# Attention scores in one VectorE pass: sum with distances, row minimum and sink together, scores divided by the slope

## The chip, the cores and the metric

The kernel runs on one core of a Trainium2 chip. A core has five engines that run on their own and wait for each other by semaphores: TensorE (PE, matrix multiply into PSUM), VectorE (DVE), ScalarE (ACT), GpSimd (POOL) and SyncE (SP, which issues DMAs). The metric is the device time of one execution in microseconds, lower is better.

## What is computed

Two transformer-like blocks on 256 tokens of width 1024, all in fp32. The change lies in the second block, in its sliding-window attention: 16 query heads of 64 share 2 key and value heads, a bias falls linearly with the distance between query and key, and each head has a sink value that takes part in the softmax as one more logit.

```python
def swa_mixer(h, w_qkv, sinks, w_o):
    ...
    s = jnp.einsum('bnqkgd,bnskd->bnkgqs', q, kb).astype(jnp.float32) * (HD ** -0.5)
    ...
    dist = BLOCK + qi - kj
    mask = (dist >= 0) & (dist < WINDOW) & (kpos >= 0)
    slopes = alibi_slopes(SWA_HEADS).reshape(1, 1, KV, G, 1, 1)
    bias = -slopes * dist.astype(jnp.float32)[None, :, None, None]
    logits = jnp.where(mask[None, :, None, None], s + bias, NEG)
    m = jnp.maximum(jnp.max(logits, axis=-1, keepdims=True), sink)
    p = jnp.exp(logits - m)
    probs = p / (jnp.sum(p, axis=-1, keepdims=True) + jnp.exp(sink - m))
    o = jnp.einsum('bnkgqs,bnskd->bnqkgd', probs.astype(vb.dtype), vb)
    return o.reshape(B_, T, SWA_HEADS * HD) @ w_o
```

BLOCK and WINDOW are 128, the slope of head n (from 1 to 16) is 2^(-n/2), and dist is the distance in tokens.

## The kernel before

Each engine has its own program, written out in order, and waits for others on counting semaphores. All weights come through one pipeline in units of 128 x 1024: SyncE loads a unit (`raw`), ScalarE copies it to a rounded high part (`whi`, line 1152), GpSimd takes the difference as the low part (`wlo`, lines 514 to 520), and TensorE does three matmuls for each product (lines 545 to 547: high by high, and the two cross terms). Six slots of each kind form the ring, so ScalarE makes the split of a unit some five units ahead.

The attention is done in eight head pairs t = 0 to 7, in a software pipeline over all engines. In order, for pair t:

- TensorE, scores (lines 1022, 1023): two heads, each 128 x 256 for the second block of tokens against both key blocks, and 128 x 128 for the first block, into the two PSUM banks `bank[0]`, `bank[1]`. All pairs use the same two banks, so the scores of pair t wait until VectorE has released those of pair t - 1 (`free("score", t)`).
- VectorE, `scores(t)` (lines 2182 to 2199): for each head one operation over 384 elements writes slope x distance minus score into `lg` (so the softmax is computed on negated values); then, behind the reciprocal of pair t - 1 (`scales(t - 1)`, line 2178), two row minima (lines 2197, 2198) over the scores and the sink column beside them, which raise `att_neg`. A masked place holds -1e30 in the table of negated distances, `ndist`.
- ScalarE (line 1562): four exponentials with their row sums, bias from the minima. Before, it has written the negated sinks into `lg` (line 1547, `att_sink`, three pairs ahead). After it, high part of an output (line 1569) and, for some t, a weight unit (line 1152).
- GpSimd (line 505): two multiplications by the reciprocals, placed in its program between weight units (lines 519, 520): pair 0, unit, pair 1, unit, pairs 2, 3 and 4, unit, pairs 5 and 6, unit, pair 7.
- TensorE, transposes (line 1038) into two PSUM banks; VectorE copies them (line 2206, `pt`); TensorE multiplies by the values (lines 1049 to 1051); ScalarE and VectorE split the result in high (line 1569) and low part (line 2212, `att_low`, which raises `att_ready`).

VectorE's order for step t is: scores(t) with the reciprocal of t - 1 in it, the copy of t - 2, the low part of t - 4. For steps 2 and 3, half of the second group of queries follows (`queries(1, ...)`, line 2154, 128 x 512). At step 7 the low part of pair 3 stands ahead of the scores. TensorE's order for step t is: scores of t, a unit of the output projection for t = 6, 8, 9 and 10 (`o_unit`, lines 545 to 547 with `ya_hi`, `ya_lo`), transposes of t - 2, values of t - 3. The first projection unit waits for the low part of pair 1, the second for that of pair 3.

`link(ins)` raises a semaphore with the instruction and has VectorE wait for it before its next one; `settle` is that wait alone.

Of the kernel before, what the change touches and what calls it, by code (L numbers as in the profile page):

```python
# [8 lines left out]
ALU = mybir.AluOpType  # L9
ACT = mybir.ActivationFunctionType  # L10
AX_X = mybir.AxisListType.X

P = 128
T = 256
# [12 lines left out]
AH = 16  # L27
AD = 64
# [10 lines left out]
C_NEG1T = C_NEG + len(LEVELS) * P  # L39
C_PICK = C_NEG1T + P  # L40
C_DIST = C_PICK + 3 * 192 + P // 2
C_ALL = C_DIST + 3 * P
EXP_TABLES = "exp_and_others"
LOG_TABLES = "natural_log_exp_and_others"
SILU_TABLES = "silu_and_others"
# [87 lines left out]
LG = 3 * P + 2  # L133
# [8 lines left out]
def build(nc, a, consts, out):  # L142
    with ExitStack() as ctx:
# [10 lines left out]
        con = sb("con", [P, C_ALL])  # L154
# [11 lines left out]
        with ExitStack() as ph:  # L166
            lg = sb("lg", [P, 3, 2 * LG], stack=ph)
# [9 lines left out]
        neg1t = con[:, C_NEG1T:C_NEG1T + P]  # L177
        pick = {s: con[:, C_PICK + 192 * i:C_PICK + 192 * (i + 1)].bitcast(I32) for i, s in enumerate((1, 4, 16))}
        pick_half = con[:, C_PICK + 3 * 192:C_DIST].bitcast(I32)
        ndist = con[:, C_DIST:C_DIST + 3 * P]  # L180


        with ExitStack() as ph:
# [45 lines left out]
        root = sb("root", [P, T])  # L229
        with ExitStack() as ph:  # L230
            qa = sb("qa", [P, KT, T], stack=ph)
            ka = sb("ka", [P, 2, T], stack=ph)
# [3 lines left out]
            st_att = sb("st_att", [P, 2, 2, 4], stack=ph)  # L236
# [118 lines left out]
        att_in = sem("att_in")  # L355
        att_neg = sem("att_neg")
# [1256 lines left out]
        def _(vec):  # L1613
            raised = {}

            def link(ins, sem_=vec_chain):

                ins.then_inc(sem_, 1)
                settle(sem_)

            def settle(sem_):

                raised[id(sem_)] = raised.get(id(sem_), 0) + 1
                vec.wait_ge(sem_, raised[id(sem_)])
# [524 lines left out]
            def queries(c, parts=range(2)):  # L2149

                group_ready("q_att", c)
                bank = pair_of("q_att", c)
                for b in parts:
                    vec.scalar_tensor_tensor(qa[:, 4 * c + 2 * b:4 * c + 2 * b + 2, :], bank[b][:, :].rearrange("p (k t) -> p k t", k=2),
                        AD ** -0.5, root[:, :].unsqueeze(1).broadcast_to([P, 2, T]), ALU.mult, ALU.mult).then_inc(att_in, 1)
                    settle(att_in)
                if b == 1:
                    free("q_att", c)

# [2 lines left out]
            queries(0)  # L2162
            group_ready("kv_att", 0)
            bank = pair_of("kv_att", 0)
            vec.tensor_tensor(ka[:, :, :], bank[0][:, :].rearrange("p (k t) -> p k t", k=2),
                root[:, :].unsqueeze(1).broadcast_to([P, 2, T]), ALU.mult).then_inc(att_in, 1)
            settle(att_in)
            link(vec.tensor_scalar(va[:, 0, :], bank[1][:, 0:P], mv[:, 0, 2:3], None, ALU.mult))
            vec.tensor_scalar(va[:, 1, :], bank[1][:, P:2 * P], mv[:, 1, 2:3], None, ALU.mult).then_inc(att_in, 1)
# [11 lines left out]
            def scores(t):  # L2181

                group_ready("score", t)
                bank = pair_of("score", t)
                par = t % 2
                if t - 2 > 0:
                    vec.wait_ge(att_t, t - 2)
                rows = lg[:, t % 3, :].rearrange("p (h c) -> p h c", h=2)
                for j in range(2):
                    blocks = bass.AP(lg, (t % 3) * 2 * LG + j * LG, [[3 * 2 * LG, P], [P + 1, 3], [1, P]])  # L2190
                    link(vec.scalar_tensor_tensor(blocks, ndist.rearrange("p (b c) -> p b c", b=3), -2.0 ** (-8.0 * (2 * t + j + 1) / AH),
                        bank[j][:, 0:3 * P].rearrange("p (b c) -> p b c", b=3), ALU.mult, ALU.subtract))
                free("score", t)
                if t > 0:
                    scales(t - 1)
                vec.wait_ge(att_sink, t + 1)
                link(vec.tensor_reduce(st_att[:, par, 0, 0:2], rows[:, :, 0:2 * P + 1], AX_X, ALU.min))
                vec.tensor_reduce(st_att[:, par, 0, 2:4], rows[:, :, 2 * P + 1:LG], AX_X, ALU.min).then_inc(att_neg, 1)
                settle(att_neg)

            def probs_turned(t):

# [123 lines left out]
def shape_constants():  # L2326

    import numpy as np

    i, j = np.arange(P)[:, None], np.arange(P)[None, :]  # L2330
    out = np.zeros((P, C_ALL), np.float32)
    out[:, C_ID:C_ID + P] = i == j
    out[:, C_UPTO:C_UPTO + P] = i <= j
    out[:, C_AFTER:C_AFTER + P] = i > j
    out[:, C_ONES:C_ONES + P] = 1
    for n, s in enumerate(LEVELS):
        below = (i // s % 2 == 1) & (j // s == i // s - 1)
        out[:, C_NEG + n * P:C_NEG + (n + 1) * P] = np.where(below, -1, 0)
        if s == 1:
            out[:, C_NEG1T:C_NEG1T + P] = np.where(below.T, -1, 0)  # L2340
    for n, s in enumerate((1, 4, 16)):
        same = np.arange(P)[:, None] // (4 * s) == np.arange(P // (4 * s))[None, :]
        block = np.arange(P) // s % 4
        rows = np.stack([block == b for b in (0, 0, 0, 1, 2, 1)], 1)
        mask = (same[:, :, None] & rows[:, None, :])[:, :, :, None].repeat(s, 3)
        out[:, C_PICK + 192 * n:C_PICK + 192 * (n + 1)] = mask.reshape(P, 192)
    out[:, C_PICK + 3 * 192:C_DIST] = np.arange(P)[:, None] < 64
    key = np.arange(2 * P)[None, :]
    dist = P + i - key
    out[:, C_DIST:C_DIST + 2 * P] = np.where((dist >= 0) & (dist < P), -dist, -1e30)  # L2350
    out[:, C_DIST + 2 * P:C_DIST + 3 * P] = out[:, C_DIST + P:C_DIST + 2 * P]
    return out


# [24 lines left out]
```

## Time and profile before

| | |
|---|---|
| median of 3 runs | 984.41 us (984.31 to 984.83) |
| the profiled execution | 984.0 us, its span 982.2 us |
| TensorE busy | 953.8 us, 97% of the span |
| GpSimd busy | 675.4 us, 69% |
| ScalarE busy | 499.4 us, 51% |
| VectorE busy | 454.7 us, 46% |

The span is from the first to the last instruction of the profile; the time of an execution is a little longer. Busy is the time in which an engine works on an instruction; an engine that is nearly always busy sets the time, and a change elsewhere counts only where this engine waits for it. The granted clock is that of TensorE, 1.0 for 2.4 GHz and 0.5 for 1.2 GHz.

### The profile page before, as it was taken

To read this page: it belongs to the slowest core of one execution; us is meant where nothing else is said; L and a number is where in the kernel's file an instruction comes from. 1 tells how busy PE (TensorE), PEld (TensorE's weight loads), DVE (VectorE), ACT (ScalarE), POOL (GpSimd) and SP (SyncE) were. 2 spreads that over 40 slices of the span, in tenths; PEclk is the share of its full clock that TensorE was granted. 3 is DMA by queue.
4 is the path that set the end of the run, shared out by engine and by line. 5 is a ranking of instruction groups with operands and counts; after the bars stand their busy time and mean duration, and the time that the engine had idled before them with its cause. 6 is when DMAs were issued, how large, how long until landed. Compare 5 with 4: busy or idle time off the path is not lost.

```text
span 982.2 us, 17653 instructions
## 1 busy us (share of the span) xinstructions
PE 953.8 (97%) x6878; PEld 893.2 (91%) x6878; DVE 454.7 (46%) x831; ACT 499.4 (51%) x702; POOL 675.4 (69%) x486
## 2 busy tenths in 40 slices
PE   6999999999999999999999999999997999999997
PEld 6999999999998889999999999888896789998886
DVE  3458753377443242666565565516537352221003
ACT  3675342573225466555566546456557346554331
POOL 4886644467555797866665676668787549889983
PEclk9999999999999999999999999999999999999999
DMA  8989858869634565644444544455572137656641
GB/s 243 167 205 108 177 103 85 157 108 101 141 106 127 182 200 167 192 129 150 132 127 129 151 130 141 135 184 175 150 235 87 49 111 226 195 171 200 206 131 43
DMA packets 131243, 146.30 MB, mean 149 GB/s; under 512 B 11022, under 2 KB 95960, under 8 KB 131160
## 3 DMA queue, kind: packets, MB, share of 16 engines
q1 hardware_dynamic: 129176, 140.64, 56.8%
q10 hardware_dynamic: 1984, 4.53, 1.4%
q8 instruction: 54, 0.88, 0.4%
q14 instruction: 29, 0.24, 0.1%
HBM read 144.10 MB, written 1.05 MB: 148 GB/s over the span
## 4 chain that ended last, share of the span: by engine, by line
PE 82%; DVE 5%; POOL 4%; issue 3%; ACT 2%; DMA 2%; SPq 1%; DVEq 0%; ACTq 0%; POOLq 0%
PE dense L545 22%; PE dense L546 21%; PE dense L547 21%; PE bank L907 3%; DMA raw<-in_w_in_even_dram 2%; POOL wlo L520 2%; PE bank L803 2%; PE bank L806 2%; POOL wlo L519 2%; PE bank L821 1%; ACT whi L1152 1%; DVE cv L1738 1%; PE bank L896 1%; PE dense L614 1%; PE bank L964 1%
## 5 line engine op out<-in xcount | busy, mean ns | idle before, releaser
L520 POOL TENSOR_TENSOR wlo<-raw,whi 128x512 fp32r<-128x512 f32 (+1 forms) x263 | 411.8, 1572 | 30.8 <-ACT whi L1152 30.8
L519 POOL TENSOR_TENSOR wlo<-raw,whi 128x512 fp32r<-128x512 f32 x199 | 258.9, 1301 | 240.2 <-ACT whi L1152 240.0
L1152 ACT ACTIVATE whi<-raw 128x1024 fp32r<-128x1024 f32 x264 | 276.3, 1058 | 274.4 <-PE dense L547 241.0
L545 PE MATMUL dense<-x_hi,whi 128*128 128x256 f32 x1232 | 360.9, 293 | 9.6 <-POOL wlo L514 4.8
L547 PE MATMUL dense<-x_hi,wlo 128*128 128x256 f32 x1232 | 348.9, 283 | 0.0
L546 PE MATMUL dense<-x_lo,whi 128*128 128x256 f32 x1232 | 348.8, 283 | 0.0
L545 PEld LDWEIGHTS dense<-x_hi,whi 128*128 128x128 f32 x1232 | 236.5, 192 | 13.2 <-issue 6.6
L546 PEld LDWEIGHTS dense<-x_lo,whi 128*128 128x128 f32 x1232 | 236.6, 192 | 1.8 <-issue 1.7
L547 PEld LDWEIGHTS dense<-x_hi,wlo 128*128 128x128 f32 x1232 | 236.2, 192 | 0.0
L545 PE MATMUL dense<-whi,ya_hi 128*128 128x512 f32 x192 | 78.5, 409 | 1.8 <-issue 1.8
L547 PE MATMUL dense<-whi,ya_lo 128*128 128x512 f32 x192 | 75.7, 394 | 0.0
L546 PE MATMUL dense<-wlo,ya_hi 128*128 128x512 f32 x192 | 75.5, 393 | 0.0
L1738 DVE SCALAR_TENSOR_TENSOR cv<-dense,colA,cv 128x255 f32<-128x255 f32 (+2 forms) x72 | 34.7, 482 | 27.1 <-ACT cv L1225 24.5
L545 PEld LDWEIGHTS dense<-whi,ya_hi 128*128 128x128 f32 x192 | 36.4, 189 | 10.0 <-issue 3.2
L547 PEld LDWEIGHTS dense<-whi,ya_lo 128*128 128x128 f32 x192 | 36.4, 189 | 7.9
L546 PEld LDWEIGHTS dense<-wlo,ya_hi 128*128 128x128 f32 x192 | 36.4, 190 | 7.2 <-issue 0.5
L1142 ACT ACT_TABLE_LOAD x32 | 41.1, 1283 | 2.4 <-PEq L2366 1.2
L545 PE MATMUL dense<-whi,x_hi 128*128 128x256 f32 (+1 forms) x144 | 40.9, 284 | 0.0
L546 PE MATMUL dense<-wlo,x_hi 128*128 128x256 f32 (+1 forms) x144 | 40.6, 282 | 0.0
L547 PE MATMUL dense<-whi,x_lo 128*128 128x256 f32 (+1 forms) x144 | 40.5, 282 | 0.0
L545 PE MATMUL dense<-whi,yb_hi 128*128 128x512 f32 x96 | 38.2, 398 | 0.3 <-POOL wlo L520 0.3
L547 PE MATMUL dense<-whi,yb_lo 128*128 128x512 f32 x96 | 37.4, 390 | 0.0
(324 smaller groups left out, 1429.4 us busy)
## 6 DMA issues: line engine op xcount, KB each, us to landing
raw<-in_w_in_odd_dram SPq DMA_DIRECT2D x64, 512.0 KB, 3.6
raw<-in_w_in_even_dram SPq DMA_DIRECT2D x32, 512.0 KB, 10.2
raw<-in_w_in_even_dram SPq DMA_DIRECT2D x64, 256.0 KB, 5.6
raw<-in_mlp_w_up_dram SPq DMA_DIRECT2D x32, 512.0 KB, 3.7
raw<-in_mlp_w_down_dram SPq DMA_DIRECT2D x32, 512.0 KB, 4.5
raw<-in_w_out_even_dram SPq DMA_DIRECT2D x16, 512.0 KB, 3.9
raw<-in_w_pl_gate_dram SPq DMA_DIRECT2D x16, 512.0 KB, 4.6
raw<-in_w_out_odd_dram SPq DMA_DIRECT2D x16, 512.0 KB, 3.9
```

The costliest lines, as they stand in the source:

```text
L519: pool.tensor_tensor(wlo[:, slot, 0:half], unit_slot(u)[:, 0:half], whi[:, slot, 0:half].bitcast(F32), ALU.subtract)
L520: pool.tensor_tensor(wlo[:, slot, first:2 * half], unit_slot(u)[:, first:2 * half], whi[:, slot, first:2 * half].bitcast(F32), ALU.subtrac ...
L545: pe.matmul(out_, lh, rh, start=start, stop=False, skip_group_check=True)
L546: pe.matmul(out_, lh, rl_, start=False, stop=False, skip_group_check=True)
L547: return pe.matmul(out_, ll, rh, start=False, stop=stop, skip_group_check=True)
L614: last = pe.transpose(bank[:, j * P:(j + 1) * P], xtok[:, t, k * P:(k + 1) * P], ident)
L803: last = pe.matmul(A[:, o], unit(LT[:, g, :], u), unit(XN[:, g, :], u), start=True, stop=True)
L806: last = pe.matmul(B[:, u * 64:(u + 1) * 64], unit(XT[:, g, :], u), even_odd(unit(EL[:, g, :], u), lv, 0), start=True, stop=True)
L907: last = pe.matmul(low_banks[:, u * T:u * T + 192], tokens_of(hk, p % 2, u // 2, u % 2), six, start=True, stop=True)
L1142: act.preload_act_table_set(name)
L1152: act.activation(whi[:, u % NSPL, :], unit_slot(u), ACT.Copy).then_inc(hi_done, 1)
L1738: link(vec.scalar_tensor_tensor(o, bank[:, i * T:(i + 1) * T - back], colA[:, w:w + 1], o, ALU.mult, ALU.add), conv_done if back == 3 else ...
```

## The change

The two operations a pair that made the biased scores and the two that took the minima become four operations, `tensor_tensor_reduce`, each of which writes (distance + score) x slope, and gives the minimum of what it wrote with the sink as the first value. For that the scores must come from TensorE as minus the score divided by the slope: the queries are multiplied by 2^t more than before, which takes one operation for each of four tiles where two tiles shared one, and the keys by a column of the constants, `nslope` (-sqrt 2 or -2 by the head within the pair). The table of distances loses its sign. Each of the new operations writes 256 elements (second block of tokens) or 128 (first block).

```diff
-C_ALL = C_DIST + 3 * P
+C_ALL = C_DIST + 3 * P + 1
...
-        ndist = con[:, C_DIST:C_DIST + 3 * P]
+        dist = con[:, C_DIST:C_DIST + 3 * P]
+        nslope = con[:, C_DIST + 3 * P:C_DIST + 3 * P + 1]
...
-                    vec.scalar_tensor_tensor(qa[:, 4 * c + 2 * b:4 * c + 2 * b + 2, :], bank[b][:, :].rearrange("p (k t) -> p k t", k=2),
-                        AD ** -0.5, root[:, :].unsqueeze(1).broadcast_to([P, 2, T]), ALU.mult, ALU.mult).then_inc(att_in, 1)
-                    settle(att_in)
+                    for j in range(2):
+                        t = 4 * c + 2 * b + j
+                        link(vec.scalar_tensor_tensor(qa[:, t, :], bank[b][:, j * T:(j + 1) * T], AD ** -0.5 * 2.0 ** t, root[:, :], ALU.mult, ALU.mult),
+                             att_in if j else vec_chain)
...
-            vec.tensor_tensor(ka[:, :, :], bank[0][:, :].rearrange("p (k t) -> p k t", k=2),
-                root[:, :].unsqueeze(1).broadcast_to([P, 2, T]), ALU.mult).then_inc(att_in, 1)
+            vec.scalar_tensor_tensor(ka[:, :, :], bank[0][:, :].rearrange("p (k t) -> p k t", k=2), nslope,
+                root[:, :].unsqueeze(1).broadcast_to([P, 2, T]), ALU.mult, ALU.mult).then_inc(att_in, 1)
...
-                rows = lg[:, t % 3, :].rearrange("p (h c) -> p h c", h=2)
+                vec.wait_ge(att_sink, t + 1)
                 for j in range(2):
-                    blocks = bass.AP(lg, (t % 3) * 2 * LG + j * LG, [[3 * 2 * LG, P], [P + 1, 3], [1, P]])
-                    link(vec.scalar_tensor_tensor(blocks, ndist.rearrange("p (b c) -> p b c", b=3), -2.0 ** (-8.0 * (2 * t + j + 1) / AH),
-                        bank[j][:, 0:3 * P].rearrange("p (b c) -> p b c", b=3), ALU.mult, ALU.subtract))
+                    slope = 2.0 ** (-8.0 * (2 * t + j + 1) / AH)
+                    row = (t % 3) * 2 * LG + j * LG
+                    for tile, first, n in ((0, 0, 2), (1, 2, 1)):
+                        o = bass.AP(lg, row + first * (P + 1), [[3 * 2 * LG, P], [P + 1, n], [1, P]])
+                        cols = slice(first * P, (first + n) * P)
+                        sink = bass.AP(lg, row + P + tile * (P + 1), [[3 * 2 * LG, P], [1, 1]])
+                        last = vec.tensor_tensor_reduce(o, dist[:, cols].rearrange("p (b c) -> p b c", b=n),
+                                                        bank[j][:, cols].rearrange("p (b c) -> p b c", b=n), slope, sink, ALU.add, ALU.min,
+                                                        accum_out=st_att[:, par, 0, 2 * tile + j:2 * tile + j + 1])
+                        link(last, att_neg if (j, tile) == (1, 1) else vec_chain)
                 free("score", t)
                 if t > 0:
                     scales(t - 1)
-                vec.wait_ge(att_sink, t + 1)
-                link(vec.tensor_reduce(st_att[:, par, 0, 0:2], rows[:, :, 0:2 * P + 1], AX_X, ALU.min))
-                vec.tensor_reduce(st_att[:, par, 0, 2:4], rows[:, :, 2 * P + 1:LG], AX_X, ALU.min).then_inc(att_neg, 1)
-                settle(att_neg)
```

The order of VectorE's instructions for step 4, with the semaphores that each waits for, is before:

```order
L2191 SCALAR_TENSOR_TENSOR lg<-con,dense 128x3x128 [waits att_in,att_t,turned]
L2191 SCALAR_TENSOR_TENSOR lg<-con,dense 128x3x128 [waits vec_chain]
L2178 RECIPROCAL rsum<-st_att 128x4 [waits vec_chain,att_scale,att_exp]
L2197 TENSOR_REDUCE st_att<-lg 128x2 [waits att_sink,att_root]
L2198 TENSOR_REDUCE st_att<-lg 128x2 [waits vec_chain]
L2206 COPY pt<-bank 128x768 [waits att_o,att_t,att_neg]
L2212 TENSOR_TENSOR ya_lo<-bank,ya_hi 128x256 [waits att_hi,att_pt]
```

And now (ISA with `lg,st_att` is the new operation, ISA with `st_att` alone the read of its accumulator):

```order
L2198 ISA lg,st_att<-con,dense,lg 128x2x128 [waits att_in,att_sink,att_t,turned]
L2198 ISA st_att 128x1
L2198 ISA lg,st_att<-con,dense,lg 128x128 [waits vec_chain]
L2198 ISA st_att 128x1
L2198 ISA lg,st_att<-con,dense,lg 128x2x128 [waits vec_chain]
L2198 ISA st_att 128x1
L2198 ISA lg,st_att<-con,dense,lg 128x128 [waits vec_chain]
L2198 ISA st_att 128x1
L2180 RECIPROCAL rsum<-st_att 128x4 [waits att_neg,att_scale,att_exp]
L2211 COPY pt<-bank 128x768 [waits att_o,att_t,att_root]
L2217 TENSOR_TENSOR ya_lo<-bank,ya_hi 128x256 [waits att_hi,att_pt]
```

Four instructions became eight, and the reciprocal moved from the middle of the score work to behind it. The program of the other engines is the same instruction by instruction, but for one DMA of the constants on ScalarE's queue, whose rows have 1025 elements instead of 1024.

The second place is the step before the scores of step 4, where half a group of queries is taken. Before:

```order
L2206 COPY pt<-bank 128x768 [waits att_t,att_neg]
L2154 SCALAR_TENSOR_TENSOR qa<-dense,root 128x512 [waits split_used,att_pt]
L2191 SCALAR_TENSOR_TENSOR lg<-con,dense 128x3x128 [waits att_in,att_t,turned]
```

And now:

```order
L2211 COPY pt<-bank 128x768 [waits att_t,att_root]
L2157 SCALAR_TENSOR_TENSOR qa<-dense,root 128x256 [waits split_used,att_pt]
L2157 SCALAR_TENSOR_TENSOR qa<-dense,root 128x256 [waits vec_chain]
L2198 ISA lg,st_att<-con,dense,lg 128x2x128 [waits att_in,att_sink,att_t,turned]
```

One operation over two tiles became two, one after the other.

## Rows read from the trace of the kernel before

**Rows 1.** The page: span, busy time of each engine, and the chain's shares.
```profile
span 982.2 us, 17653 instructions
...
PE 953.8 (97%) x6878; PEld 893.2 (91%) x6878; DVE 454.7 (46%) x831; ACT 499.4 (51%) x702; POOL 675.4 (69%) x486
...
PE 82%; DVE 5%; POOL 4%; issue 3%; ACT 2%; DMA 2%; SPq 1%; DVEq 0%; ACTq 0%; POOLq 0%
```

**Rows 2.** Busy time by stage; columns: length, engines, clock, DMA share, GB/s.
```profile
740.00:758.00 18.00, 12.33 (x101) 9.85 (x100) 15.33 (x28) 12.51 (x40) 14.25 (x15) 0.97 0.25 81
```

**Rows 3.** Timeline of VectorE; columns: start, duration (of all in xN), instruction, idle before.
```profile
741.84 0.69 DVE L2154 SCALAR_TENSOR_TENSOR qa<-dense,root 128x512 f32<-128x512 f32 x1
...
747.21 1.15 DVE L2191 SCALAR_TENSOR_TENSOR lg<-con,dense 128x384 f32<-128x384 f32 x2 [0.21 <-DVE qa L2154]
748.57 0.18 DVE L2178 RECIPROCAL rsum<-st_att 128x4 f32<-128x4 f32 x1 [0.21 <-DVE lg L2191]
748.78 0.69 DVE L2197 TENSOR_REDUCE st_att<-lg 128x2 f32<-128x514 f32 x1
749.51 0.42 DVE L2198 TENSOR_REDUCE st_att<-lg 128x2 f32<-128x258 f32 x1
749.96 0.96 DVE L2206 COPY pt<-bank 128x768 f32<-128x768 f32 x1
...
755.15 0.42 DVE L2212 TENSOR_TENSOR ya_lo<-bank,ya_hi 128x256 fp32r<-128x256 f32 x1
...
763.03 1.15 DVE L2191 SCALAR_TENSOR_TENSOR lg<-con,dense 128x384 f32<-128x384 f32 x2
```

**Rows 4.** Timeline of TensorE from the first projection unit on.
```profile
755.68 0.47 PE L545 MATMUL dense<-whi,ya_hi 128*128 128x512 f32 x1 [1.83 <-issue]
...
757.42 0.63 PE L545 MATMUL dense<-whi,ya_hi 128*128 128x512 f32 x1
...
759.99 0.93 PE L1038 MATMUL bank<-con,lg 128*128 128x128 f32 x6
...
767.52 0.82 PE L1038 MATMUL bank<-con,lg 128*128 128x128 f32 x6
...
773.88 0.88 PE L1038 MATMUL bank<-con,lg 128*128 128x128 f32 x6 [1.49 <-POOL lg L505]
```

**Rows 5.** Timeline of ScalarE and GpSimd behind the scores of pair 7.
```profile
765.84 0.51 ACT L1562 ACTIVATE lg<-lg,st_att 128x257 f32<-128x257 f32 x1 [3.37 <-DVE st_att L2198]
...
764.65 1.61 POOL L505 TENSOR_TENSOR lg<-lg,rsum 128x512 f32<-128x512 f32 x2 [5.81 <-DVE rsum L2178]
...
769.72 1.30 POOL L519 TENSOR_TENSOR wlo<-raw,whi 128x512 fp32r<-128x512 f32 x1 [3.46 <-ACT whi L1152]
...
772.22 1.61 POOL L505 TENSOR_TENSOR lg<-lg,rsum 128x512 f32<-128x512 f32 x2
```

**Rows 6.** Groups of VectorE by line (busy, mean ns), then a stretch of ScalarE's timeline.
```profile
L1738 DVE SCALAR_TENSOR_TENSOR cv<-dense,colA,cv 128x255 f32<-128x255 f32 x24 | 11.6, 483 | 25.3 <-ACT cv L1225 24.5
L2304 DVE SCALAR_TENSOR_TENSOR zt<-xtok,mv,gb 128x512 f32<-128x512 f32 x2 | 1.5, 752 | 0.6 <-ACT mv L1604 0.6
L2212 DVE TENSOR_TENSOR ya_lo<-bank,ya_hi 128x256 fp32r<-128x256 f32 x8 | 3.4, 425 | 6.3 <-ACT ya_hi L1569 6.1
...
731.72 0.51 ACT L1562 ACTIVATE lg<-lg,st_att 128x257 f32<-128x257 f32 x1 [5.07 <-DVE st_att L2198]
732.13 0.19 ACT L1562 ACTIVATION_READ_ACCUMULATOR lg<-lg,st_att 128x1 f32 x1
732.35 0.51 ACT L1562 ACTIVATE lg<-lg,st_att 128x257 f32<-128x257 f32 x1
```

**Rows 7.** VectorE's wait, the constants' first DMA, and TensorE's clock by stage.
```profile
725.45 0.69 DVE L2165 TENSOR_TENSOR ka<-dense,root 128x512 f32<-128x512 f32 x1 [8.99 <-PE dense L547]
con<-shape_constants_dram ACTq DMA_DIRECT2D x1, 64.0 KB, 3.3
757.00:758.00 1.00, 1.00 (x4) 0.50 0.00 0
```

More of the change, by code:

```diff
@@ L2349, in shape_constants @@
     dist = P + i - key
-    out[:, C_DIST:C_DIST + 2 * P] = np.where((dist >= 0) & (dist < P), -dist, -1e30)
+    out[:, C_DIST:C_DIST + 2 * P] = np.where((dist >= 0) & (dist < P), dist, 1e30)
     out[:, C_DIST + 2 * P:C_DIST + 3 * P] = out[:, C_DIST + P:C_DIST + 2 * P]
+    out[:, C_DIST + 3 * P] = np.where(np.arange(P) < 64, -2.0 ** (8.0 / AH), -2.0 ** (16.0 / AH))
     return out
```

## The prediction

> **What bounds the kernel now.** Read the page first: TensorE is busy 97% of the 982.2 us and holds 82% of the chain that ended last [rows 1]. A change on VectorE counts only where TensorE waits. The change lies between 725 and 770 us, and the busy time by stage shows that this is the one stretch where TensorE is not full: 12.33 us of 18 between 740 and 758, with VectorE busy 15.33 [rows 2].
>
> In order of time, VectorE works without a real pause from 741.84 on, in blocks of one head pair: two score operations, the reciprocal of the pair before, two row minima, the copy of turned scores, the low part of an output [rows 3]. TensorE's output projection cannot start before the low part of pair 1, which runs 755.15 to 755.57; its first matmul stands at 755.68 [rows 3, 4]. After it come the transposes of pair 4 (759.99), its values and the scores of pair 7, all back to back. VectorE takes pair 7 at 763.03, ScalarE its exponentials at 765.84, then a weight unit; GpSimd splits that unit at 769.72 and scales pair 7 only at 772.22; TensorE, idle by then, turns pair 7 at 773.88 [rows 3 to 5]. From there its work is dense. So two VectorE times set the end: when the low part of pair 1 is done, and when the minima of pair 7 are done.
>
> **The change, part by part.** One number for a pause between two linked operations: 748.78 + 0.69 to 749.51 and 749.51 + 0.42 to 749.96 leave 0.04 and 0.03; I take 0.035 us [rows 3].
>
> *Removed per pair:* two score operations and two minima. From 747.21 to 749.96 is 2.75 us, of which 748.36 (= 747.21 + 1.15) to 748.78 is the reciprocal with its pause, 0.42. Score work: 2.33 us.
>
> *Added per pair:* four operations of 256, 128, 256 and 128 elements, each with an accumulator read. Each operation has one PSUM input, one SBUF input and a per-partition scalar (the sink). The nearest row has just this make-up: 255 elements, 483 ns [rows 6]. An element costs (689 - 422)/256 = 1.04 ns, from the two minima of 514 and 258 elements [rows 3]. So 484 and 350 ns, with pauses 2 x (0.484 + 0.350 + 0.07) = 1.81 us. The read of VectorE's accumulator is in no row. Above it stands the smallest operation here, the reciprocal, 0.18 + 0.035 = 0.21. ScalarE's accumulator read is nearest in kind: 0.19 long, but it starts 0.41 after an operation of 0.51, and the next starts 0.63 after the first, so it adds 0.63 - 0.51 - 0.02 = 0.10 [rows 6]. Below that nothing but full overlap, 0. I take 0.15, between the two near rows, since each next operation waits for the read. Score work after: 1.81 + 4 x 0.15 = 2.41 us; bounds 2.21 and 2.65, and 1.81 with the reads free. That is +0.08 a pair: two passes became one, but four fixed costs became eight.
>
> *Queries:* each operation over 512 elements becomes two over 256. One with its pause is 0.69 + 0.035 = 0.73 now; two of 0.425 (the 256-element low part) with pauses are 0.92, +0.18 [rows 3, 6]. Two of them (before pairs 3 and 4) are on the path, +0.37. Those of the first half are hidden: VectorE idles 9 us behind them, until the keys' group is done [rows 7]. The keys' operation gains a scalar, about 0.06 (752 ns with a scalar against 0.69 without, at 512 elements [rows 3, 6]); the unit of query matmuls that TensorE does before the first scores hides it; without that cover it costs its 0.06.
>
> *Moved:* the reciprocal, and the release of the score banks, now come after the minima. The minima of pair 7 therefore stop waiting for a reciprocal: -0.42 on the path. The reciprocal starts 2.41 + 0.21 after the block instead of 1.36, 1.26 later. Who waits for it is GpSimd's scaling, then the transposes. For pair 6 scaling ends at 764.65 + 1.61 = 766.26 and the transposes start at 767.52 behind a projection unit: 1.26 of cover, just used up, and another 1.5 us of TensorE idle before 773.88 behind it [rows 4, 5]. For pair 3 the reciprocal would start at 748.57 + 0.45 (one block and both query parts) + 1.26 = 750.3, and scaling end 0.18 + 1.61 later, at 752.1. The banks are released at the end of block 5, near 751.9 + 2.4 = 754.4; the scores of pair 6 then take some 0.9, and the low part of pair 1 comes at 756.2 (755.57 + 0.61). Covered by 0.9. Queued on VectorE behind the four operations are the reciprocal and the copy; the sink values they wait for were written one to several pairs earlier. ScalarE's and GpSimd's order does not change.
>
> *Sum.* Blocks 3, 4 and 5 lie before the low part of pair 1: 3 x 0.08 + 0.37 = +0.61. Block 7: 0.08 - 0.42 = -0.34. Together +0.27 us; in general four times the score work less 9.37 (3 x 2.33 + 2.75 - 0.37). With 2.21 it is -0.5, with 2.65 +1.2, with free reads -2.1. The profiled execution took 984.0 (982.2 and 1.8 around it), so 984.3; the runs' median is 984.41, so 984.7 in the unit of the runs.
>
> **A rate.** The operation at 512 elements with two SBUF inputs and a scalar takes 752 ns, (512 x 1.04) + 219, so it runs at one element a cycle like the others [rows 6]. Against this stands the Trainium skill, "Vector Engine (DVE) Microarchitecture Reference", section 7 (Points that are easy to get wrong): a scalar_tensor_tensor shape with two non-bf16 SBUF sources has half the throughput, for want of a port for the accumulator. By that rule the time would be the 987.9 of the first rival; by the row it stays at 984.7. Here one source is in PSUM, and no row of before accumulates on VectorE, so the trace does not settle it.
>
> **The rivals.**
> 1. *Half rate.* The new operation takes two cycles an element. 768 elements a pair cost 0.80 us more; on four blocks 3.2, so 987.9. For it: it does three things in one pass and carries a value from element to element. Against it: the minima carry one too and run at full rate. It decides from 0.5 us a pair. This is the case of slower. Chance 0.08.
> 2. *The clock does not fall.* At 757 the granted clock went from 1.0 to 0.5, after a pause of TensorE of 1.83 us before the projection; until 759.99 the last seven matmuls of the unit, of 512 columns, stood 0.43 apart (from 757.42 to 759.99 are six), twice what they take at full clock [rows 4, 7]. In the changed kernel the pause is split by the later scores of pair 6. If the fall stays out, 7 x 0.21 = 1.5 us come off: 983.2. Chance 0.20.
> 3. *The clock falls for longer or once more,* say over the next projection unit's 12 matmuls: 12 x 0.21 = +2.5, 987.2. Pauses on TensorE grow a little everywhere. Chance 0.07.
> 4. *The reads are free:* 982.3. Against it is that each next operation waits for the read. Chance 0.06.
> 5. *The late reciprocal binds,* because GpSimd is late for the transposes: needs 2.8 us of lateness for pair 6, or 0.9 more than reckoned for pair 3, where each 0.1 above costs 0.1; about 986. Chance 0.04.
> 6. *The start.* The constants' rows get one element longer in memory, and TensorE's first transposes need the first of them. That transfer took 3.3 us [rows 7]; a tenth more is +0.3, 985.0. Chance 0.05.
>
> My forecast, clock as before and reads between 0.10 and 0.21, has 0.50: 983.9 to 985.6.
>
> **How the numbers follow.** The predicted time is 984.7. What a measurement of this kernel can tell from no change is 0.2%, 2.0 us, so the forecast and cases 2, 5 and 6 are within it. Slower takes case 1, most of case 3 and mixtures with costly reads: 0.16. Faster takes half of case 4 and case 2 with cheap reads: 0.06. Same: 0.78. The range leaves out case 1, part of 3 and part of 4: 982.8 to 986.9.
>
> **What would show it.** In the profile after: the 256-element operation 0.48 us and the 128-element one 0.35, reads near 0.15 apart; if not, case 1 or 4. Score work near 2.4 a pair. The first projection matmul near 756.3. The minima of pair 7 end 2.4 after its start. VectorE busy time about the same, TensorE's idle between the projection's third unit and pair 7's transposes still there. The clock row at 757 to 760 tells cases 2 and 3. What would make the prediction wrong is a read of over 0.3 us, a rate below one element a cycle, or a fall of the clock elsewhere.

## Result and the profile after

| | median us | lowest to highest |
|---|---|---|
| before | 984.62 | 984.31 to 987.08 (4 runs) |
| changed | 974.08 | 973.64 to 976.7 (4 runs) |

The ratio is 0.9893, with an interval of 0.9869 to 0.9917: 10.5 us faster. The prediction had 984.7 us, a range from 982.8 to 986.9, and gave "faster" 0.06. It was wrong, and by more than any case it had named.

The page of the changed kernel, against [rows 1]: the span is 10.3 us shorter, and TensorE's own busy time is 9.6 us shorter, with the same 6878 instructions. The change took no instruction from TensorE, so a wait that went away can't be the whole story.

```profile
span 971.9 us, 17687 instructions
...
PE 944.2 (97%) x6878; PEld 880.7 (91%) x6878; DVE 451.1 (46%) x867; ACT 499.6 (51%) x702; POOL 675.4 (69%) x486
```

**Where the time went.** Follow one instruction that both programs have. `root` is copied right before the first attention query, ahead of every changed operation, and once more behind the attention; its row gives both starts. Before, then after:

```profile
L2147 DVE COPY root<-bank x2: 425/425/425, 714.6 to 807.3; 128x256 f32<-128x256 f32 x2
```

```profile
L2148 DVE COPY root<-bank x2: 425/425/425, 710.3 to 799.2; 128x256 f32<-128x256 f32 x2
```

4.3 us were gained before any of the changed operations had run. Up to the second copy it is 8.1, at the end 10.3: 4.3 ahead of the attention, 3.7 to 3.8 in it, 2.2 behind it. The prediction had looked only at the middle part.

**In the attention.** VectorE's timeline of the changed kernel at step 2 (start, duration, instruction), then one whole block at step 3, against the block from 747.21 to 749.96 in [rows 3]:

```profile
732.82 0.48 DVE L2198 CUSTOM_DVE_ANT_0 lg<-con,dense,lg 128x256 f32<-128x256 f32 x1 [1.85 <-PE dense L1024]
...
738.34 0.48 DVE L2198 CUSTOM_DVE_ANT_0 lg<-con,dense,lg 128x256 f32<-128x256 f32 x1
738.75 0.08 DVE L2198 DVE_READ_ACCUMULATOR2_ANT st_att<- 128x1 f32 x1
738.87 0.35 DVE L2198 CUSTOM_DVE_ANT_0 lg<-con,dense,lg 128x128 f32<-128x128 f32 x1
739.14 0.08 DVE L2198 DVE_READ_ACCUMULATOR2_ANT st_att<- 128x1 f32 x1
739.26 0.48 DVE L2198 CUSTOM_DVE_ANT_0 lg<-con,dense,lg 128x256 f32<-128x256 f32 x1
739.66 0.08 DVE L2198 DVE_READ_ACCUMULATOR2_ANT st_att<- 128x1 f32 x1
739.78 0.35 DVE L2198 CUSTOM_DVE_ANT_0 lg<-con,dense,lg 128x128 f32<-128x128 f32 x1
740.05 0.08 DVE L2198 DVE_READ_ACCUMULATOR2_ANT st_att<- 128x1 f32 x1
740.35 0.18 DVE L2180 RECIPROCAL rsum<-st_att 128x4 f32<-128x4 f32 x1 [0.21 <-DVE st_att L2198]
740.56 0.96 DVE L2211 COPY pt<-bank 128x768 f32<-128x768 f32 x1
```

The operations last 0.48 and 0.35 us, as reckoned. But each read of the accumulator starts 0.41 (0.27) after the start of its operation, before the end that the profile gives that operation, and the next operation starts 0.12 after the read. From start to start an operation with its read takes 0.53 and 0.39, one head 0.92. The block is 2.22 long instead of 2.75; less the reciprocal's 0.42 the score work is 1.80 us, not 2.41.

TensorE's timeline after, against [rows 4]:

```profile
750.14 0.48 PE L546 MATMUL dense<-whi,ya_hi 128*128 128x512 f32 x1 [0.67 <-issue]
750.45 0.40 PE L547 MATMUL dense<-wlo,ya_hi 128*128 128x512 f32 x1
750.69 0.39 PE L548 MATMUL dense<-whi,ya_lo 128*128 128x512 f32 x1
...
753.01 0.82 PE L1039 MATMUL bank<-con,lg 128*128 128x128 f32 x6
...
765.87 0.88 PE L1039 MATMUL bank<-con,lg 128*128 128x128 f32 x6 [0.51 <-POOL lg L506]
```

The pause before the projection is 0.67 us instead of 1.83, and behind the first matmul the others of the unit stand 0.23 to 0.24 apart. The 12 matmuls take 2.87 us (750.14 to 753.01) instead of 4.31 (755.68 to 759.99). The clock stays at its upper level (1.00, 2.4 GHz) through the whole stage; before, it was 0.50 from 757 to 760 [rows 7]. Here are the stage after, with its clock in the last column but two, and the three microseconds before:

```profile
740.00:760.00 20.00, 17.20 (x138) 13.86 (x137) 15.11 (x50) 13.74 (x47) 11.82 (x14) 1.00 0.19 59
```

```profile
757.00:760.00 3.00, 3.00 (x9) 2.25 (x8) 1.26 (x3) 1.51 (x5) 1.73 (x3) 0.50 0.50 160
```

ScalarE's exponentials of pair 7 and GpSimd's scaling follow 8.0 us earlier than in [rows 5]:

```profile
757.84 0.51 ACT L1563 ACTIVATE lg<-lg,st_att 128x257 f32<-128x257 f32 x1 [2.45 <-DVE st_att L2198]
```

```profile
764.20 1.62 POOL L506 TENSOR_TENSOR lg<-lg,rsum 128x512 f32<-128x512 f32 x2
```

**Outside the attention.** A run of ordinary projection matmuls near 130 us, of before and of after (starts in the first column):

```profile
132.08 0.28 PE L547 MATMUL dense<-x_hi,wlo 128*128 128x256 f32 x1
132.20 0.28 PE L545 MATMUL dense<-x_hi,whi 128*128 128x256 f32 x1
132.32 0.28 PE L546 MATMUL dense<-x_lo,whi 128*128 128x256 f32 x1
132.44 0.28 PE L547 MATMUL dense<-x_hi,wlo 128*128 128x256 f32 x1
132.56 0.28 PE L545 MATMUL dense<-x_hi,whi 128*128 128x256 f32 x1
```

```profile
130.06 0.28 PE L546 MATMUL dense<-x_hi,whi 128*128 128x256 f32 x1
130.18 0.28 PE L547 MATMUL dense<-x_lo,whi 128*128 128x256 f32 x1
130.30 0.28 PE L548 MATMUL dense<-x_hi,wlo 128*128 128x256 f32 x1
130.41 0.28 PE L546 MATMUL dense<-x_hi,whi 128*128 128x256 f32 x1
130.53 0.28 PE L547 MATMUL dense<-x_lo,whi 128*128 128x256 f32 x1
130.65 0.28 PE L548 MATMUL dense<-x_hi,wlo 128*128 128x256 f32 x1
130.76 0.28 PE L546 MATMUL dense<-x_hi,whi 128*128 128x256 f32 x1
```

Four steps of 0.12 there, six steps in 0.70 here: 120 ns from start to start against 117, for the same matmul of the same 256 columns. There are 4080 matmuls of 256 columns with `x_hi` or `x_lo`. The one thing in the diff that can reach them is `C_ALL`: `con` has 2561 columns instead of 2560, the allocation rounds up, and in the compiled program every tile in SBUF behind `con` starts 32 bytes later in its partition. The tiles `whi` and `wlo` lie ahead of `con` and stay.

### The profile page after: what moved, and what is told of

It is laid out like the page before. It is cut to its first block, busy times and chain, and to the rows that moved or that the text cites. A ratio compares the mean times of both kernels' runs of the same rounds, so it can differ in the third digit from the quotient of the medians.

```text
span 971.9 us, 17687 instructions
## 1 busy us (share of the span) xinstructions
PE 944.2 (97%) x6878; PEld 880.7 (91%) x6878; DVE 451.1 (46%) x867; ACT 499.6 (51%) x702; POOL 675.4 (69%) x486
## 3 DMA queue, kind: packets, MB, share of 16 engines
HBM read 144.10 MB, written 1.05 MB: 149 GB/s over the span
## 4 chain that ended last, share of the span: by engine, by line
PE 85%; DVE 4%; POOL 3%; ACT 3%; DMA 2%; issue 2%; SPq 1%; DVEq 0%; ACTq 0%; POOLq 0%
PE dense L546 23%; PE dense L547 22%; PE dense L548 22%; PE bank L908 3%; DMA raw<-in_w_in_even_dram 2%; PE bank L804 2%; PE bank L807 2%; POOL wlo L521 1%; POOL wlo L520 1%; PE bank L822 1%; POOL lg L506 1%; DVE cv L1739 1%; PE bank L897 1%; ACT whi L1153 1%; PE dense L615 1%
## 5 line engine op out<-in xcount | busy, mean ns | idle before, releaser
L546 PE MATMUL dense<-x_hi,whi 128*128 128x256 f32 x1232 | 356.9, 290 | 11.1 <-POOL wlo L515 5.3
L547 PE MATMUL dense<-x_lo,whi 128*128 128x256 f32 x1232 | 344.5, 280 | 0.0
L548 PE MATMUL dense<-x_hi,wlo 128*128 128x256 f32 x1232 | 344.3, 279 | 0.0
L546 PEld LDWEIGHTS dense<-x_hi,whi 128*128 128x128 f32 x1232 | 232.4, 189 | 14.8 <-issue 7.4
L547 PEld LDWEIGHTS dense<-x_lo,whi 128*128 128x128 f32 x1232 | 232.4, 189 | 1.8 <-issue 1.7
L548 PEld LDWEIGHTS dense<-x_hi,wlo 128*128 128x128 f32 x1232 | 232.1, 188 | 0.0
```

The costliest lines, as they stand in the source:

```text
L546: pe.matmul(out_, lh, rh, start=start, stop=False, skip_group_check=True)
L547: pe.matmul(out_, lh, rl_, start=False, stop=False, skip_group_check=True)
L548: return pe.matmul(out_, ll, rh, start=False, stop=stop, skip_group_check=True)
```

## Theories

**A (addresses).** The spacing of matmuls depends on where the tiles of their two operands start; the shift of 32 bytes gives what lies outside the attention. **S (scores).** The operations give what lies in it: shorter score work, and a clock that does not fall. **Rival:** nothing but S, with the rest due to the constants' longer rows in DRAM or to chance.

## Experiments

"Spacing" below is the median distance of the starts of neighbouring matmuls in the trace: `x` for the products of moving `x_hi` or `x_lo` (256 columns) with the weights as the stationary tile, `ya` for those of the weights (moving, 512 columns) with `ya_hi` or `ya_lo` as the stationary tile (`yb` and `p` alike unless said), `ac` the same for the MLP's. "The attention stretch" runs from the start of TensorE's scores of pair 2 (736.10 before) to that of the transposes of pair 7 (773.88). Each ratio is to the kernel before on the same chip. The first four ran on one chip.

**e1_before_pad32: the shift alone.**

```diff
         con = sb("con", [P, C_ALL])
+        pad = sb("pad", [P, 8])
```

> The kernel before with nothing changed but an unused 32-byte tile behind the constants, so that every tile from colA on starts 32 bytes later, as in the changed kernel. Theory A (the time of a matmul depends on where its operands' tiles start within 64 bytes): x_hi matmuls 117 ns apart instead of 120, those with ya or yb 233 instead of 227, ac 227 instead of 234; the attention stage is reached 4.3 us earlier and the end gains another 2.4: 977.9 us, with no change inside the attention stage. Rival B (the early gain comes from the constants' longer rows in memory, from the added operation's table or from chance): 984.4 us. Rival C (the whole gain is that of the score operations): 984.4 us.

Measured: 980.85 us (977.23 to 983.86, 10 runs; before 985.74), ratio 0.9948 (0.9928 to 0.9968); the profiled span 975.4, 6.8 below before. Spacings 117, 233 to 234, 227, as in the changed kernel. The root copies' stretches: 4.3 us shorter up to the first, 2.2 from the second to the end; the attention stretch 37.82 us against 37.79. Theory A holds for what lies outside, without one changed operation. The spacings add up, too: 4080 matmuls at 3 ns less make 12.2 us, 912 with `ya`, `yb` and `p` at 6 more 5.5 us, and 186 with `ac` at 7 less 1.3 us, together 8.0 us less; TensorE's busy time in this run is 945.8 us, 8.0 less than before.

**e2_after_nopad: the operations alone.** `nslope` in a tile of its own behind all others, written by two memsets; the constants at 2560 columns.

```diff
-C_ALL = C_DIST + 3 * P + 1
+C_ALL = C_DIST + 3 * P
...
+        nslope = sb("nslope", [P, 1])
...
+            for n in range(2):
+                link(vec.memset(nslope[64 * n:64 * n + 64, :], -2.0 ** (8.0 * (n + 1) / AH)))
```

> The changed kernel with the tiles where they were before: the keys' factor stands in a tile of its own behind all others, set by two small VectorE operations, and the constants have their old size. Theory A: matmuls 120, 227 and 234 ns apart as before, the stage reached at its old time, 3.7 us saved between pair 2's scores and pair 7's transposes (2.1 from the shorter score work, 1.5 from the clock that does not fall): 980.7 us. Rival B or C: 974.1 us, or B with the gain in the constants' rows: 980.7 with the new spacings kept.

Measured: 981.15 us (980.22 to 983.1), 0.9956 (0.9943 to 0.997). Spacings as before; the attention stretch 34.16 us, 3.6 shorter; clock not fallen. In the profile the first copy of `root` comes 0.7 us later than before, so nothing is gained ahead of the attention. Theory S holds for the middle. The product of both ratios, 0.9904, lies within the interval of the change.

**e3_before_row2561: the constants' rows alone.** In DRAM one column more, in SBUF the layout of before; the last of the constants' DMAs still moves 1024 elements a row, not 1025 as in the changed kernel.

> The kernel before with the constants' rows in memory 2561 elements long instead of 2560, all tiles on chip as before. Theory A: 984.4 us, or up to 0.65 more, since the first unit's matmul stood 0.65 later in the changed kernel (12.03 against 11.38). Rival B (longer rows bring the early gain): 980 or less.

Measured: 985.23 us, 0.9996 (0.9982 to 1.0009). The longer rows make no difference that can be told from noise. Nor does the one element more in that DMA: e1, without it, reaches the first copy of `root` at 710.26 us and the changed kernel at 710.27. With e1 and e3 the rival falls.

**e4_before_pad64: twice the shift** (`pad` of 16 floats, 64 bytes).

> The kernel before with an unused 64-byte tile behind the constants, so that every later tile moves by 64 bytes. Theory A with a period of 64 bytes: 984.4 us and the spacings of before (120, 227, 234 ns). If the period is 128 bytes or longer, or any shift acts, the x_hi spacing is 117 or another value than 120.

Measured: 983.49 us, 0.9983 (0.9968 to 0.9997). Spacings 118, 233, 233, where before has 120, 227, 234: a shift by 64 bytes does not give the old spacings back, so 64 bytes is no period of the effect.

**e5_after_layout and e6_before_layout: a layout by design.** I thought that 512 columns go fast from a multiple of 128 bytes: `x` moved by 32 bytes, `ya`, `yb`, `p`, `ac` to multiples of 256; with the operations of after and of before. These and the next two ran on a second chip.

```diff
+        pad_x = sb("pad_x", [P, 8])
         x_hi = sb("x_hi", [P, KT, T], F32R)
         x_lo = sb("x_lo", [P, KT, T], F32R)
+        pad_y = sb("pad_y", [P, 24])
         ya_hi = sb("ya_hi", [P, KT, T], F32R)
...
+        pad_ac = sb("pad_ac", [P, 8])
```

> The changed score operations (keys' factor in a tile of its own) with a layout chosen by what the first runs showed: x_hi and x_lo start 32 bytes past a multiple of 128, ya, yb, p and ac start on a multiple of 128. Theory A (the start within 128 bytes sets the spacing: a 256-column moving operand is faster off it, a 128-column stationary operand under 512 moving columns is faster on it): 117 for x_hi, 227 for ya, yb, p and ac at once. From 984.4: 4080 matmuls x 3 ns = 12.2 off, 192 x 6.5 = 1.3 off, 0.8 of it lost where TensorE waits, and 3.6 off in the attention stage: 968 us. Rival D (x_hi and ya share one property that can't be had for both, such as the distance between the two operands): no better than 974.

> The same layout with the score operations of before. Theory A: 984.4 - 12.7 = 971.7 us, 3.6 above the kernel with the changed score operations. Rival D: not below 977.

Measured: 976.37 us (0.9901, 0.9881 to 0.992) and 979.87 (0.9933, 0.9912 to 0.9955), before 985.47. Spacings 117, 232, 232. Expected were 227 for `ya` and `ac`, and 968 and 971.7 us, so my form of theory A fell: a multiple of 128 is not enough. That the two stand 3.5 us apart confirms S once more.

**e7_before_whi32: the weights moved too.** `whi` and `wlo` 32 bytes later, everything behind them at another offset again.

```diff
+        pad_w = sb("pad_w", [P, 8])
         whi = sb("whi", [P, NSPL, SPLK * COLS], F32R)
         wlo = sb("wlo", [P, NSPL, SPLK * COLS], F32R)
         con = sb("con", [P, C_ALL])
+        pad_c = sb("pad_c", [P, 24])
```

> The kernel before with whi and wlo alone starting 32 bytes past a multiple of 128 and everything else as it was. It exchanges the roles: for x_hi the stationary operand is off and the moving one on, for ya the moving one off and the stationary one on. Theory A: x_hi slower than 120 ns (the stationary operand costs 3 or more), ya 227 or less; 984.4 + 12 or more = 997 us. Rival D (only the difference of the two starts counts): x_hi 117 and ya 233, 978 us.

Measured: 990.36 us (988.8 to 993.57), 1.0048 (1.0026 to 1.0071), slower than before. The distances of `x` spread from 115 to 126 ns here, with a mean of 120 as before; `ya` and `ac` stand 234 to 235 apart. Neither theory A (997 us) nor D as it was worded (`x` 117, 978 us) gave this. The slower `ya`, `yb` and `p` account for it: 912 matmuls times 6 to 7 ns are about 6 us, and 4.9 were measured (990.36 - 985.47).

**e8_after_nopad_slow: score work made long again.** e2 with one more VectorE operation of 384 elements per pair, into a tile that nothing reads. It makes the score work 2.42 us, which is what the prediction had thought.

```diff
+                        if (j, tile) == (1, 0):
+                            link(last)
+                            link(vec.tensor_tensor(idle[:, :], dist, bank[0][:, 0:3 * P], ALU.add))
+                            continue
```

> The changed kernel with the old addresses and one more VectorE operation a pair, between the last two score operations: distances plus scores of 384 elements into a tile that nobody reads, 0.59 us with its pause. It makes the score work 1.83 + 0.59 = 2.42 us a pair, what the prediction had put at 2.41. Theory S (the prediction's chain was right and only the accumulator read was mis-sized): four times 0.59 = 2.4 us back, so 983.1, and another 1.5 us if the granted clock falls again at the first projection unit: 984.6. Rival E (other waits set the stage and the score work is hidden): 981.2, as without it.

Measured: 985.21 us (983.47 to 988.15), 0.9993 (0.9979 to 1.0007): with the predicted score work and the old addresses the time is that of before. The attention stretch is 36.96 us, 2.8 above e2, where the work alone makes 4 x 0.6 = 2.4. That the remaining 0.4 is the clock's is likely, but no run separates it: the clock fell here, elsewhere than before, at a pause of 2.13 us, and stayed at 1.00 at the projection, whose pause is now split into parts of 0.38 and 0.81 us by the scores of pair 6. TensorE's row at the fall, and the clock by stage:

```profile
744.72 1.54 PE L1040 MATMUL bank<-con,lg 128*128 128x128 f32 x6 [2.13 <-POOL lg L507]
```

```profile
745.00:748.00 3.00, 3.00 (x18) 2.49 (x17) 2.63 (x8) 1.73 (x7) 3.00 (x3) 0.50 0.29 111
```

**What the starts had in common.** By now it looked as if the start of the activations' tile (`x`, `ya`, `yb`, `p`, `ac`) counted against that of the weights' tile, both modulo 256 bytes. Three more kernels, with the changed kernel beside them, ran on a third chip (before 985.72 us).

**e9_before_all32: everything shifted together**, `pad_w` of 8 floats ahead of `whi` and nothing else.

> The kernel before with 32 unused bytes per partition right ahead of whi, so that whi, wlo and every tile behind them start 32 bytes later together (whi, wlo, x_hi, ya_hi, yb_hi, p_hi at 160 modulo 256, ac_hi at 128). If what counts is how the moving tile starts against the weights' tile (theory D), x and ya keep the spacing of before (120 ns for 256 columns, 227 ns for 512) and the time is 984 to 985 us. If what counts is the moving tile's own start (theory M), x goes to 117 ns, ya, yb and p to 233, ac to 227, and the time is that of e1, 978 to 981 us. If it is the weights' start alone, x and ya stay at 120 and 233 ns as in e7, about 990 us.

Measured: 985.72 us (983.8 to 986.88), 0.9995 (0.9981 to 1.001); spacings 120, 227, 234. `x_hi`, `ya_hi` and `ac_hi` start just where they do in the changed kernel, and their matmuls behave as before. Not the start of one tile counts but how the two stand to each other (form D of the expectation). The other two forms fell.

**e10_after_layout2 and e12_before_layout2: the best of each**, with the changed operations (from e2) and with those of before. Both have these three tiles:

```diff
+        pad_x = sb("pad_x", [P, 8])
         x_hi = sb("x_hi", [P, KT, T], F32R)
         x_lo = sb("x_lo", [P, KT, T], F32R)
+        pad_y = sb("pad_y", [P, 56])
         ya_hi = sb("ya_hi", [P, KT, T], F32R)
...
+        pad_ac = sb("pad_ac", [P, 8])
```

> The changed operations in a layout that takes the better spacing of each tile as seen so far: whi, wlo at 128 modulo 256 as before, x_hi and x_lo 32 bytes later (160), ya, yb and p back at 128, ac at 128. Expected by both forms D and M: x 117 ns, ya, yb, p and ac 227 ns. Against the changed kernel 912 matmuls of 512 columns become 6 ns shorter, 5.5 us of TensorE, so 966 to 970 us if TensorE is the bound there, and 974 if other work bounds those stages. If only the whole shift by 32 bytes of everything behind con brings the gain, it is 978 or more.

> The operations of before in the layout of e10. If addresses and operations add up, it stands above e10 by what the operations alone brought in the other two pairs (984.6 to 981.2 and 979.9 to 976.4, that is 3.5 us): 970 to 974 us, faster than the changed kernel or equal to it without any of its operations. If the gain of addresses is only that of e1, it is 978 to 981.

**e11_after_again: the changed kernel on that chip.**

> The changed kernel itself, on the same chip as e10 and e12, to compare with them: 974 us, ratio to before 0.989.

Measured: e10 970.87 us (969.34 to 972.49), 0.9839 (0.9811 to 0.9866); e12 974.42 (972.36 to 976.1), 0.9873 (0.9845 to 0.9902); e11 974.99 (974.46 to 979.44), 0.9892 (0.9853 to 0.9931). e10 and e12 lie 0.9 and 0.4 us above the ranges expected by form D (966 to 970 and 970 to 974), and well under the 978 us and more expected without it. e10 is the fastest kernel of the study, 4.1 us under the changed one, and all of its runs are below the lowest of e11. e12 has not one changed operation and is as fast as the change: three unused tiles do as much. Operations and addresses add up again, 3.6 us between e10 and e12.

TensorE is busy for 940.5 us in e10, against 944.2 in the changed kernel and 953.8 before. Groups of matmuls by shape (count, busy us, mean ns) of before, after, e9 and e10:

```profile
L546 PE MATMUL dense<-x_lo,whi 128*128 128x256 f32 x1232 | 348.8, 283 | 0.0
L546 PE MATMUL dense<-wlo,yb_hi 128*128 128x512 f32 x96 | 37.4, 389 | 0.0
L546 PE MATMUL dense<-wlo,ac_hi 128*128 128x512 f32 x62 | 24.5, 395 | 0.0
```

```profile
L547 PE MATMUL dense<-x_lo,whi 128*128 128x256 f32 x1232 | 344.5, 280 | 0.0
L547 PE MATMUL dense<-wlo,yb_hi 128*128 128x512 f32 x96 | 37.9, 395 | 0.0
L547 PE MATMUL dense<-wlo,ac_hi 128*128 128x512 f32 x62 | 24.1, 389 | 0.0
```

```profile
L547 PE MATMUL dense<-x_lo,whi 128*128 128x256 f32 x1232 | 349.0, 283 | 0.0
L547 PE MATMUL dense<-wlo,yb_hi 128*128 128x512 f32 x96 | 37.4, 389 | 0.0
L547 PE MATMUL dense<-wlo,ac_hi 128*128 128x512 f32 x62 | 24.5, 395 | 0.0
```

```profile
L550 PE MATMUL dense<-x_lo,whi 128*128 128x256 f32 x1232 | 344.6, 280 | 0.0
L550 PE MATMUL dense<-wlo,yb_hi 128*128 128x512 f32 x96 | 37.4, 389 | 0.0
L550 PE MATMUL dense<-wlo,ac_hi 128*128 128x512 f32 x62 | 24.1, 389 | 0.0
```

In these four kernels each kind of matmul has two values, 3 ns apart for 256 columns and 6 for 512. The changed kernel won on `x`, lost on `yb` and won on `ac`; e10 has the better value in all three, e9 the old one in all three.

All layouts side by side (start modulo 256 bytes; spacing in ns):

| kernels | whi | x | ya, yb, p | ac | x spacing | ya | ac |
|---|---|---|---|---|---|---|---|
| before, e2, e3, e8 | 128 | 128 | 128 | 96 | 120 | 227 | 234 |
| after, e1, e11 | 128 | 160 | 160 | 128 | 117 | 233 to 234 | 227 |
| e4 | 128 | 192 | 192 | 160 | 118 | 233 | 233 |
| e5, e6 | 128 | 160 | 0 | 0 | 117 | 232 | 232 |
| e7 | 160 | 0 | 0 | 224 | 120 (115 to 126) | 234 | 235 |
| e9 | 160 | 160 | 160 | 128 | 120 | 227 | 234 |
| e10, e12 | 128 | 160 | 128 | 128 | 117 | 227 | 227 |

With equal starts the 512-column matmuls are at their best and the 256-column ones at their worst; every other distance tried is worse for the former, and for the latter better, but for e7, where the mean is as it was.

## Why the prediction was wrong, point by point

**The failed step** is the scope of the sum: it had terms for the operations and, of the one new constants column, only "The constants' rows get one element longer in memory". It priced the DMA (which costs nothing, e3) and put at nothing, without a reason, the 32 bytes by which every later tile moves. They are as large a part as the operations: e1, the shift alone, took 4.9 us off the median. "What bounds the kernel now" had set out from "A change on VectorE counts only where TensorE waits" and looked between 725 and 770 us alone; that is right for VectorE's work, and the diff changed something on TensorE as well.

**The mis-sized term** is the accumulator read: 0.15 us taken, 0.10 to 0.21 as bounds, free reads left to a rival. It added 0.01 us at most (0.53 from start to start, where operation and pause alone make 0.52), and the score work was 1.80 instead of 2.41. By the prediction's own formula 4 x 1.80 - 9.37 = -2.17 instead of +0.27. "Each next operation waits for the read" was true, but the read itself runs inside the time that the profile gives to the operation. Rival 4, held at 0.06, is what happened.

**Rival 2, the clock,** held at 0.20, came true as worked out (-1.5), with a pause of 0.67 instead of 1.83 us before the projection. Its reason was that the later scores of pair 6 would split that pause, and e8, with the predicted score work, does show this: no fall at the projection. But its clock falls at 744.7, at a pause of 2.13 us. At that place the operations of before have a pause of 2.19 us, and there the profiles differ: no fall in that of before, one in e3 with the same addresses (0.50 from 745 to 748). So e8 shows that a fall can come elsewhere, as the prediction's last sentence had allowed; whether that one hangs on the length of the score work stays open. At the projection the profiles agree: all five with the short score work (after, e2, e5, e10, e11) keep 1.00 over the whole stage, and all eight with the old operations, at whatever addresses, have the pause of 1.83 us and the fall. Such a one is e12; its stage around the projection's start:

```profile
750.00:755.00 5.00, 4.16 (x11) 3.35 (x12) 3.11 (x7) 3.28 (x12) 3.88 (x4) 0.66 0.32 96
```

Together the two rivals make -2.17 - 1.5 = -3.7; the stretch from VectorE's (not TensorE's) scores of pair 2 to the transposes of pair 7 shrank by 3.67 (36.72 from 737.16 to 773.88 before, 33.05 from 732.82 to 765.87 after). The prediction had priced each of them alone, 982.3 and 983.2; both together were in no case of their own, and its range ended at 982.8.

The start of VectorE's scores of pair 2 before, for this difference:

```profile
737.16 1.15 DVE L2191 SCALAR_TENSOR_TENSOR lg<-con,dense 128x384 f32<-128x384 f32 x2 [1.27 <-PE dense L1023]
```

**Right:** the durations of the new operations (0.48 and 0.35 us against 0.484 and 0.350), the form of the sum, and that the late reciprocal is covered (rival 5 did not come). From VectorE's scores of pair 2 to the first projection matmul it is 18.52 us before and 17.32 after: -1.20, where three blocks of -0.53 and the queries' +0.37 make -1.22. For the keys' operation, the row of after has 751 ns against 0.69 us before:

```profile
L2167 DVE SCALAR_TENSOR_TENSOR ka<-dense,con,root x1: 751/751/751, 721.2 to 721.2; 128x512 f32<-128x512 f32 x1
```

**Rival 1, half rate,** did not come. The groups of the new operation, by shape:

```profile
L2198 DVE CUSTOM_DVE_ANT_0 lg<-con,dense,lg 128x256 f32<-128x256 f32 x16 | 7.7, 482 | 6.8 <-PE dense L1024 6.1 <-ACT lg L1548 0.3
L2198 DVE CUSTOM_DVE_ANT_0 lg<-con,dense,lg 128x128 f32<-128x128 f32 x16 | 5.6, 348 | 0.6
```

482 less 348 ns over 128 elements is 1.05 ns an element, as in the other rows (1.04), so the rate is not halved. The Trainium skill's sentence on half throughput ("Vector Engine (DVE) Microarchitecture Reference", section 7) is about two SBUF sources. The new operation has one in PSUM, and the row of `zt` in [rows 6], with two in SBUF at full rate, gives out no accumulated value, so no run here tests the sentence for an operation that does both.

**Still open, in part:** why equal starts hurt one kind of matmul and help the other. The two kinds differ in which operand moves (`x` moves and the weights are stationary; with `ya` the weights move) and in the columns (256 and 512). The traces separate these: for some products `x` is the stationary tile and 256 columns of the weights move. Of before, after and e9:

```profile
L546 PE MATMUL dense<-wlo,x_hi 128*128 128x256 f32 x128 | 36.2, 283 | 0.0
```

```profile
L547 PE MATMUL dense<-wlo,x_hi 128*128 128x256 f32 x128 | 36.0, 281 | 0.0
```

```profile
L547 PE MATMUL dense<-wlo,x_hi 128*128 128x256 f32 x128 | 36.2, 283 | 0.0
```

Their spacing is 120 ns with equal starts (before, e9) and 117 in the changed kernel, so at 256 columns equal starts are the worst whichever tile moves; the sign goes with the columns. The size does depend on which one moves: with `x` 64 bytes off (e4) it is 118 ns for moving `x` and 114 for moving weights, in e7 120 and 117. Why all this is so, no run shows.

e1's runs spread from 977.23 to 983.86 us, and the granted clock goes with it: the mean was 0.998 in its two fastest runs, and the two runs at 0.992 took 981.47 and 982.93. At 0.998 the kernel before took 983.84 to 985.13 on that chip, 6.5 to 7.9 us more than e1, which fits the 6.8 of the spans; at 0.996 the difference of the medians is 4.6 (984.43 and 979.82), and over all runs it is 4.9 (985.74 - 980.85). Why the shift is worth less when the clock falls more often stays open.

## What to carry to other kernels

Compare an instruction that both programs have and that lies ahead of the change before explaining anything: here it alone showed that 4.3 us came from elsewhere. A change of a tile's size moves every tile allocated behind it; in a kernel bound by TensorE try layouts by themselves, with unused tiles, and separate them from the edit whose worth you want to know. Price an operation with its accumulator read by the distance to the next start, not by the sum of two durations.

## What the runs showed of the hardware

- The distance between matmul starts depends on how the start of the moving tile in SBUF stands to that of the stationary one: with equal starts modulo 256 bytes 120 ns for 256 columns, else 117 or 118 (but 120 for moving `x` in e7, and 114 for moving weights in e4); with equal starts 227 for 512 columns, else 232 to 235, at full clock. Over the layouts tried the same operations of before ran from 974.42 us (e12) to 990.36 (e7).
- VectorE's accumulator read is 0.08 us long and starts 0.41 us into an operation shown as 0.48; the next operation starts 0.12 us after the read's start.
- The granted clock fell to 0.50 at a pause of TensorE of 1.83 us (before) and of 2.13 us (e8), and did not at one of 0.67 us (after) at the place of the first. A pause does not settle it alone: before had one of 2.19 us at 743.79 and kept its clock, and in e3 the clock fell at that place.
